# Modulation vectors of a ten-section transformer kernel: from GpSimd multiply and add to VectorE multiply-adds, with GpSimd only issuing their loads

## What is computed

```python
m = cond @ w_mod[l] + b_mod[l]            # 1024 -> 3 * 1024 for each section
h = rmsnorm(x, g) * (1 + m_scale) + m_shift
x = x + m_gate * branch(h)
```

## Time and profile before

| what | value |
|---|---|
| median of 3 runs | 4373.36 us (4373.17 to 4393.44) |
| profiled execution: its own time, its span | 4384.72 us, 4382.9 us |
| TensorE busy, mean granted clock | 4127.2 us (94%), 0.966 |
| VectorE busy | 2579.5 us (59%), 3627 instructions |
| ScalarE busy | 1469.6 us (34%) |
| GpSimd busy | 1062.1 us (24%), 640 instructions |
| GpSimd's 189 additions at line 636 | 2776 ns each on average |
| GpSimd's 216 loads, median from issue to landing | 4.4 us |
| HBM traffic | 802 MB read, 183 GB/s over the span |

### The profile page before, as it was taken

One profiled execution on the slowest core, in us unless ns is written; L12 is line 12 of the kernel. 1 busy time (PEld: TensorE's weight loads), 2 busy tenths in 40 slices (PEclk: granted clock), 3 DMA queues, 4 the chain that ended last, 5 costly groups with the idle time before them and its releaser, 6 DMA issues.

```text
span 4382.9 us, 73959 instructions
## 1 busy us (share of the span) xinstructions
PE 4127.2 (94%) x29877; PEld 3942.5 (90%) x29877; DVE 2579.5 (59%) x3627; ACT 1469.6 (34%) x2008; POOL 1062.1 (24%) x640
## 2 busy tenths in 40 slices
PE   5998999987999888999999999998889999999999
PEld 3996899965898778999999999987789999999999
DVE  6845577653865645955555555546445555555555
ACT  1422334311431233333333333311323333333333
POOL 3836466561747402700000000070000000000000
PEclk8998999988999998999999999999989999999999
DMA  6764576751776324756556556563235565565564
GB/s 235 267 204 152 181 257 202 242 182 45 232 235 222 123 77 142 264 191 197 181 190 197 182 190 196 188 218 109 78 115 183 190 196 182 191 197 181 191 197 141
DMA packets 569488, 804.87 MB, mean 184 GB/s; under 512 B 20973, under 2 KB 487860, under 8 KB 568100
## 3 DMA queue, kind: packets, MB, share of 16 engines
q1 hardware_dynamic: 514364, 665.69, 46.7%
q0 software_dynamic: 31104, 113.26, 7.5%
q10 hardware_dynamic: 23912, 24.44, 1.7%
HBM read 802.13 MB, written 1.20 MB: 183 GB/s over the span
## 4 chain that ended last, share of the span: by engine, by line
PE 86%; DVE 10%; issue 2%; ACT 1%; DMA 1%; SPq 0%; DVEq 0%; ACTq 0%
PE bank L742 22%; PE bank L743 22%; PE bank L744 22%; PE bank L839 10%; DVE work L1841 2%; PE bank L1048 2%; PE bank L737 1%; PE bank L723 1%; DVE ring_lo L1606 1%; DVE pb L1752 1%; DVE work L1705 1%; DMA ring<-in_ffn_w 0%; DVE hid L1634 0%; PE bank L1034 0%; DMA ring<-in_w_mod 0%
## 5 line engine op out<-in xcount | busy, mean ns | idle before, releaser
L742 PE MATMUL bank<-hh,hi 128*128 128x256 f32 (+1 forms) x5568 | 1581.8, 284 | 16.4 <-issue 12.3
L743 PE MATMUL bank<-h_lo,hi 128*128 128x256 f32 (+1 forms) x5568 | 1580.9, 284 | 0.0
L744 PE MATMUL bank<-hh,ring_lo 128*128 128x256 f32 (+1 forms) x5568 | 1580.8, 284 | 0.0
L742 PEld LDWEIGHTS bank<-hh,hi 128*128 128x128 f32 (+1 forms) x5568 | 1070.5, 192 | 17.6 <-issue 13.4
L743 PEld LDWEIGHTS bank<-h_lo,hi 128*128 128x128 f32 (+1 forms) x5568 | 1070.4, 192 | 0.0
L744 PEld LDWEIGHTS bank<-hh,ring_lo 128*128 128x128 f32 (+1 forms) x5568 | 1070.2, 192 | 0.0
L1602 DVE TENSOR_TENSOR ring_lo<-ring,hi 128x1024 fp32r<-128x1024 f32 (+1 forms) x696 | 866.2, 1284 | 131.7 <-ACT hi L1183 131.4
L742 PE MATMUL bank<-hid,hi 128*128 128x256 f32 (+1 forms) x2784 | 789.3, 284 | 9.2 <-DVE hid_lo L1636 9.0
L744 PE MATMUL bank<-hid,ring_lo 128*128 128x256 f32 (+1 forms) x2784 | 788.4, 283 | 0.0
L743 PE MATMUL bank<-hid_lo,hi 128*128 128x256 f32 (+1 forms) x2784 | 788.4, 283 | 0.0
L1183 ACT ACTIVATE hi<-ring 128x1024 fp32r<-128x1024 f32 (+1 forms) x696 | 694.4, 1044 | 276.8 <-DMA ring<-in_ffn_w 134.3
(11 more groups left out here) (254 smaller groups left out, 3071.6 us busy)
## 6 DMA issues: line engine op xcount, KB each, us to landing
ring<-in_w SPq DMA_DIRECT2D x384, 1024.0 KB, 5.6
ring<-in_ffn_w SPq DMA_DIRECT2D x120, 1024.0 KB, 7.6
wmod<-in_w_mod POOLq DMA_DIRECT2D x216, 512.0 KB, 4.4
ring<-in_w_in SPq DMA_DIRECT2D x74, 1024.0 KB, 5.5
ring<-in_w_out SPq DMA_DIRECT2D x16, 1024.0 KB, 6.1
work<-gates_scratch ACTq DMA_DIRECT2D x128, 128.0 KB, 5.2
ring<-in_w_mod SPq DMA_DIRECT2D x12, 1024.0 KB, 16.7
ring<-in_ffn_w SPq DMA_DIRECT2D x12, 768.0 KB, 5.1
```

The costliest lines, as they stand in the source:

```text
L742: pe.matmul(o, w_hi, x_hi, start=start, stop=False, skip_group_check=True)
L743: pe.matmul(o, w_hi, x_lo, start=False, stop=False, skip_group_check=True)
L744: return pe.matmul(o, w_lo, x_hi, start=False, stop=stop, skip_group_check=True)
```

## The change

VectorE makes the partial sums now, as multiply-adds in one instruction: `scalar_tensor_tensor` on 128x1024 (a `tensor_scalar` for the first of each third), 24 steps for each of sections 1 to 9. GpSimd keeps its first part (section 0's gate) and then only issues the 216 loads, each after the step that frees its half of `wmod`. The order of the steps is now by row group first and third second.

In a stage of tiles the steps stand between the tiles of the last five double units, one or two for each tile, and all 24 are placed by then. In a mixer all 24 stand together ahead of the head norms. The partial sums for sections 1, 4, 6 and 8 go to a part of `work` (`mod_work`), the others to `macc`. The load of the attention bias (`bias`, 1.5 MB) moves from the end of section 0 to behind section 1's norm, since it overlaps `mod_work`. The ring begins with slot 0 in all stages from section 3 on; before, sections 5, 7 and 9 began with slot 3.

```diff
-                ringplan.align(0 if s == 3 else 3)
+                ringplan.align(0 if s >= 3 else 3)
...
+        MOD_STEPS = 3 * KD
+        def mod_at(q):
+            return 1 + q // MOD_STEPS, q % MOD_STEPS // 3, q % 3
...
+            for q in range(MOD_STEPS * (SECTIONS - 1)):
...
+                if q >= 2:
+                    pool.wait_ge(mod_step, q - 1)
+                pool.dma_start(wmod[:, q % 2, :], w[l][k][:, at:at + D]).then_inc(mod_full[q % 2], 16)
...
+            def add_mods(count, upto):
+                for q in range(mod_next[0], min(mod_next[0] + count, upto)):
...
+                    dve.wait_ge(mod_full[q % 2], 16 * (q // 2 + 1))
+                    if k == 0:
+                        dve.tensor_scalar(acc, w, c, None, ALU.mult).then_inc(mod_step, 1)
+                    else:
+                        dve.wait_ge(mod_step, q - 2)
+                        dve.scalar_tensor_tensor(out=acc, in0=w, scalar=c, in1=acc, op0=ALU.mult, op1=ALU.add).then_inc(mod_step, 1)
+                    mod_next[0] = q + 1
...
+                        add_mods(min(mods, 1), steps_to)
...
+                    add_mods(mods - 1, steps_to)
...
+                for i in range(n // 2 - 1 - UNROLLED, n // 2):
+                    two_units(i, i == n // 2 - 1, 2 if steps_to and i % 2 else 1 if steps_to else 0)
...
+                add_mods(MOD_STEPS, MADE_IN[s][1])
                 head_norms(X, tiles(PROJ, 5), 4, 1, qgain[:, 0:1] if ab else qgain[:, 1:2], col(gname, 1), tiles(RS1, 5))
```

More of the change, by code:

```diff
@@ L278, in build @@
         ring_lo = rounded("ring_lo", [P, RING, SLAB], "ring")
+        mod_work = tiles(32, 12).rearrange("p a t -> p (a t)")
         gates = tiles(66, 2)
@@ L329, in build @@
         mod_full = [sem(f"mod_full{i}") for i in range(2)]
-        mod_seen = sem("mod_seen")
-        mod_scaled, mod_step, mod_summed = sem("mod_scaled"), sem("mod_step"), sem("mod_summed")
+        mod_step, mod_summed = sem("mod_step"), sem("mod_summed")
         first_mod = sem("first_mod")
@@ L488, in build, with mod_sums @@
               for s in range(SECTIONS)]
+        MOD_STEPS = 3 * KD
+        def mod_at(q):
+            return 1 + q // MOD_STEPS, q % MOD_STEPS // 3, q % 3
+        def mod_sums(n):
+            return mod_work if n in (1, 4, 6, 8) else macc
+        MADE_IN = {0: (0, 24), 1: (24, 48), 2: (48, 72), 3: (72, 96), 4: (96, 120), 5: (120, 144), 6: (144, 168), 7: (168, 192), 8: (192, 216)}
         SMALL_LOADS = sum(2 if n in HALF_ROWS else 1 for g in GROUPS for n, _ in g)
@@ L608, in _ @@
         def _(pool):
[L609 to L640, removed]
             pool.wait_ge(cond_done, 2)
@@ L655, in _ @@
             pool.wait_ge(first_gate, KD)
[L656 to L661, removed]
+            wm1 = A["w_mod"].rearrange("l (p k) m -> l k p m", p=P)
+            wm2 = A["w_mod_2"].rearrange("l (p k) m -> l k p m", p=P)
+            for q in range(MOD_STEPS * (SECTIONS - 1)):
+                n, k, third = mod_at(q)
+                w, l, i = (wm1, n // 3, n % 3) if n < 6 else (wm2, (n - 6) // 2, n % 2)
+                at = i * MODS + third * D
+                if q >= 2:
+                    pool.wait_ge(mod_step, q - 1)
+                pool.dma_start(wmod[:, q % 2, :], w[l][k][:, at:at + D]).then_inc(mod_full[q % 2], 16)
         @block.tensor
@@ L734, in sum_mods @@
                 else:
-                    pe.wait_ge(mod_step, 3 * KD * n)
+                    pe.wait_ge(mod_step, MOD_STEPS * n)
                 for j in range(MODT):
-                    ins = pe.matmul(bank[3][:, j:j + 1], macc[:, j * P:(j + 1) * P], M["ones"][:, 0:1], start=True, stop=True)
+                    ins = pe.matmul(bank[3][:, j:j + 1], mod_sums(n)[:, j * P:(j + 1) * P], M["ones"][:, 0:1], start=True, stop=True)
                 ins.then_inc(mod_summed, 1)
@@ L1126, in setup_loads, with load_bias @@
                 act.dma_start(axial[:, :, :].rearrange("p a t -> p (a t)"), A["k_axial"]).then_inc(consts_in, 16)
+            def load_bias():
+                act.wait_ge(window_out, 17)
+                act.wait_ge(mod_summed, 2)
+                act.dma_start(bias, bass.AP(window_dram, 0, [[1, P], [512, NQ], [1, 384]])).then_inc(bias_in, 16)
             def load_router(l):
@@ L1426, in _ @@
                 norm(sec)
+                if s == 1:
+                    load_bias()
                 if s == 6:
@@ L1480, in add_mod @@
                     dve.scalar_tensor_tensor(out=acc, in0=w, scalar=c, in1=acc, op0=ALU.mult, op1=ALU.add).then_inc(first_mod, 1)
+            mod_next = [0]
+            def add_mods(count, upto):
+                for q in range(mod_next[0], min(mod_next[0] + count, upto)):
+                    n, k, third = mod_at(q)
+                    acc, w = mod_sums(n)[:, third * D:(third + 1) * D], wmod[:, q % 2, :]
+                    c = cond[:, (0 if n < 6 else KD) + k:(0 if n < 6 else KD) + k + 1]
+                    dve.wait_ge(mod_full[q % 2], 16 * (q // 2 + 1))
[5 more added lines that the diff above has]
+                    mod_next[0] = q + 1
             def setup():
@@ L1648, in units, with two_units @@
                 lo_down(odd[2], 0, down_count(sec, 6, 0))
-                def two_units(i, last):
+                UNROLLED = 4
+                steps_to = MADE_IN[s][1] if s in MADE_IN else 0
+                def two_units(i, last, mods=0):
                     tile, u6 = i * 4 + (t0 + 2), i * 12
@@ L1654, in expert @@
                         if not moe:
[L1655 to L1658, removed]
+                            hidden(t, tile + (2 * v + t))
+                        else:
+                            if t == 0:
+                                dve.wait_ge(gates_in[v], i * 16 + (gates0 + 16))
+                            hidden(t, tile + (2 * v + t), gate=gates[:, v, :], gated_count=i * 4 + (sec["gated0"] + 2 * v + t + 1))
+                        add_mods(min(mods, 1), steps_to)
                     expert(0, 0)
@@ L1677, in two_units @@
                         lo_down(odd[2], 0, down_count(sec, u6 + 18, 0))
-                with dve.Fori(0, n // 2 - 1) as i:
-                    two_units(i, False)
-                two_units(n // 2 - 1, True)
+                        add_mods(mods - 1, steps_to)
+                if n // 2 - 1 > UNROLLED:
+                    with dve.Fori(0, n // 2 - 1 - UNROLLED) as i:
+                        two_units(i, False)
+                for i in range(n // 2 - 1 - UNROLLED, n // 2):
+                    two_units(i, i == n // 2 - 1, 2 if steps_to and i % 2 else 1 if steps_to else 0)
+                add_mods(MOD_STEPS, steps_to)
                 banks0 = 3 * sum(plan[r]["kind"] in ("ffn", "moe") for r in range(s))
```

2 lines of the change are left out of this document (removed).

## The result

The changed kernel takes 4420.46 us (median of six runs, 4409.72 to 4428.42). Six runs of the kernel before, on the same chip, have a median of 4384.44 (4373.17 to 4393.44). The ratio is 1.0087, with an interval of 1.0065 to 1.0109: slower by 36 us, or 0.9%. The profiled execution of the changed kernel took 4427.8 us, 43.1 more than that of before.

The account below looks back on a forecast made before the run. TensorE was taken as the limit in stages of tiles, with VectorE on the path in the four mixers. 124.7 - 65.1 - 14.4 - 5.7 = +39.5 us on 4373.4 gave 4413 us, range 4366 to 4450.

Parts of the forecast that it names:

- what is added: Start of the four mixers: 24 steps in a row, paced by their loads, delay sections 1, 4, 6 and 8: +124.7 us.
- what is taken away: In the four mixers GpSimd no longer holds up VectorE's operations: -65.1 us.
- The cycle's parts: Mixers: step 1.2, GpSimd's wake 0.30, landing 5.0 or 4.0, VectorE's wake 0.2; cycles of 6.7 and 5.7 us.
- How far TensorE is late: Mixers: delays of 42.8, 41.8, 24.8 and 15.3 us in sections 1, 4, 6 and 8.
- the cover by slabs: Sections 6 and 8: TensorE's slabs cover part of the steps' delay, leaving 24.8 and 15.3 us.
- The ring: Section 5's start: its first slab gets a slot free earlier, so TensorE's norm waits less: -14.4 us.
- The stages of tiles: Section 7's start becomes like section 9's, 5.7 us saved; steps inside the stages of tiles cost nothing.
- cover of about a tile: Stages of tiles: VectorE prepares weights about a tile ahead of TensorE; without that 24 steps would cost 29 us.
- The first: Mixers: loads land as if alone, at 3.5 us; sign turns at about 3.9 us; 4356 us; 20% for 4356 to 4385.
- The second: Stages of tiles: VectorE becomes late and TensorE loses 12 us; 4425 us; 7%.
- the fourth: Section 5's start: the ring gives nothing, since something else holds the norm; 4427 us; 5%.
- The third: Mixers: VectorE's step holds up the next load's issue, 44 cycles by 0.9 us, 40 us; 4453 us; 8%.

Follow-up runs that it names:

- ring-alone kernel: The kernel before with only the new ring order (stages from section 3 on begin with slot 0): 4368.53 us against 4381.08, ratio 0.9973.
- the old ring: The changed kernel with the ring order of the kernel before put back: 4437.22 us, ratio to before 1.0125.
- the doubled steps: The changed kernel with 21 of the 24 multiply-adds in each of sections 0, 2, 3, 5 and 7 done a second time: 4427.9 us, ratio to before 1.0102.

## Why the prediction was right, and where its terms were off

The forecast was 4413 us with steps at the pace of their loads, on a base of 4373.4. The later runs put that base at 4384.4, and the result at 4420.5: my base, a median of three, was 11.0 us low (the profiled execution lies 0.3 us above the later median, not 11.3). Between the medians it is +36.0, between the two profiled executions +43.1 where I had +39.5, and in the sections of the table +41.3. That the sum is so near is in part luck, since its misses cancel: what is added came out 11.3 us larger than I had it, and what is taken away 9.5 larger (3.2 of hold, 3.5 of ring, 2.8 of tiles).

- **What is added, 24 steps in a row.** Right in kind: VectorE's idle time is put down to the `wmod` loads, and taking these away gives back 133 us. The term of +124.7 measures 136.0. The cycle's parts: the step 1.28 where I had 1.2, GpSimd's wake 0.30 as said, VectorE's wake under 0.1 in place of 0.2, the landing 5.3 beside slabs (I took 5.0) and 3.9 without (4.0). The row of 24 is 76.7 us in section 1 for 72.1. The first cycle there lasts 321.45 - 313.26 = 8.2 us: the first two loads were issued within 2 us of the attention bias's 1.5 MB and had a median of 8.0 us. Section 4 has no such load and its row is 75.7, so my estimate is that the bias is worth about a microsecond of the 4.6. The third cycle is as long as the first, 336.71 - 328.50 = 8.2; the rest is landings beside slabs longer than my 5.0.
- **How far TensorE is late.** The head norms of section 1 begin at 389.96 in place of "near 384"; 2 us of the 6 is the start of the program. Section 4 follows the same count. In sections 6 and 8 the cover by slabs was counted right: 25.3 for 24.8, and 18.4 for 15.3. In section 6 the rotation itself begins only 20.6 us later in the section than before: the tables ahead of the steps, free of GpSimd, end 4.5 us sooner, a gain that stands in no term of mine.
- **What is taken away.** -65.1 measures -68.3, or -66.9 by the ring-alone kernel. Section 1 was worth 16.2 where I had 10.5, but 8.4 by that kernel; section 4 23.8 for 25.7. The rope's multiply at 0.69 us holds in section 4 too:

```profile
1015.05 0.69 DVE L1720 TENSOR_TENSOR work<-work,axial 128x512 f32<-128x512 f32 x1 [2.24 <-PE bank L843]
...
1020.78 1.19 DVE L1745 COPY kz<-work 64x256 f32<-64x256 f32 x4
```

  These answer to the 2.00 and 4.62 us of the earlier trace rows; the copies' 1.19 is the 1.2 of the prediction.
- **The ring.** -14.4 measures -13.9 within the change and -18.0 in the kernel before: the mechanism is shown by the norm's wait of 1.74 us (1.82 with the ring alone, 14.13 with the old ring), the size only to some 4 us.
- **The stages of tiles.** -5.7 measures -8.5 in section 7, and 0 in the others. The stretch I had it from gives 5.6: TensorE is busy 151.15 of 160 us from 1741 us on. That the steps cost nothing was right; the reason, cover of about a tile, was too careful: twice the steps cost nothing in four stages and 1.9 us in section 7.
- **The rivals.** The first needed landings under 3.9 us; beside slabs they were 5.3. The second fell with the doubled steps, the fourth with both kernels on the ring. The third said that VectorE's other step holds up the next issue. The trace of the changed kernel speaks against it: at 345.19 GpSimd issues in the midst of the second step (344.93 to 346.21), 0.30 us after the first, and this load and the next one, issued with VectorE idle, land alike, at 5.3 us each. By the Trainium skill, "SBUF — State Buffer", the section on the two separate sides, an operation with two SBUF inputs blocks GpSimd only where GpSimd reads SBUF itself; the trace agrees. No run was made for it alone, and the first step of each third, a multiply, is not covered by this reading.

What I had not weighed is the alternative that the change left open. The wait is not the price of VectorE doing the steps, but of their standing in a row at the one place of a mixer where nothing covers a landing. Dealt out over the mixer, the same steps with the same loads, ring and tiles included, give 89 us.

## What to carry to other kernels

A chain of steps that each need their own load runs at the pace of the landing (here about 5 us for 1.3 us of work); before moving such steps to another engine, count the gaps in that engine's work that are as long as a landing, and place one or two steps at each. A step is cheap on a busy engine and dear on a critical one: 45 steps in a stage whose dense stretches had VectorE 98% busy cost 0 to 1.9 us, and 24 in a mixer, where it had been busy for 37% to 49% of the time, cost 18 to 48 us. Where a change has a gain and a loss in one section, as section 8 has 18.0 against 18.4 us, take away the one alone, since the net of 0.4 us looks like nothing happened.

## What the runs showed of the hardware that I had not expected

- Four loads of 256 KB in flight land little sooner than two of 512 KB: 5.1 us and 5.3 beside slabs, 3.2 and 3.9 without. By the Trainium skill, "DMA: Bandwidth & Descriptors", the section on the anatomy of one SWDGE DMA, such a load takes about 2.0 us and its bytes at 436 KB per us, so an estimate of 2.6 and 3.2 us; without slabs 512 KB took 3.9, and beside slabs 256 and 512 KB took 2.5 and 2.1 us more than their estimates. The page's figure for 256 KB is for one load, and no run here has one alone.
- The first step of a modulation, a multiply alone, takes 0.75 us, and a multiply-add of the same 128x1024 elements 1.28.
- In a stretch of 34 us of section 0 TensorE loses nothing with VectorE busy for 98% of it; in one of 35 us of section 7, also at 98%, it loses 0.89 us.
- A pause costs TensorE more than its length. After 20.23 us of idle time the eight rotations of section 6 ran at a granted clock of 0.50 for their first 3.28 us and took 6.50 us in all; without a pause, before and with the steps dealt out, they took 3.60. The mean clock of a whole section says less: section 1 has 0.79 after the change and 0.86 before, with TensorE busy for 153.2 and 156.3 us, since most of the difference falls into the pause.
